# A streaming encoder step on one core: filling TensorE's opening and taking the first forget and query products feature by feature

## The reference

```python
x = layer_norm(x, ln_in_g, ln_in_b)
proj = einsum('btd,dn->btn', x, w_in)
q, f_pre, i_v, g_o, u_a, u_b, gate_a, gate_b = split(proj)
logf = log_sigmoid(f_pre) + log1p(lb * exp(-f_pre))   # 8 heads of 128 columns
...                                                   # gated recurrence over blocks of 64 frames
mix = (sigmoid(gate_a) * A + sigmoid(gate_b) * B) @ w_out
x = layer_norm(alpha * x + mix)
x = layer_norm(alpha * x + moe(x))                    # 16 experts, the best 2 of one group
```

## Time and profile before

| | us |
|---|---|
| median of 3 runs | 857.52 (857.51 to 860.41) |
| profiled execution | 857.89 |
| its span | 856.0 |
| TensorE busy | 812.6 (95%) |
| VectorE busy | 423.0 (49%) |
| ScalarE busy | 239.4 (28%) |
| GpSimd busy | 84.2 (10%) |

### The profile page before, as it was taken

One profiled execution on the slowest core, in us unless ns is written; L12 is line 12 of the kernel. 1 busy time (PEld: TensorE's weight loads), 2 busy tenths in 40 slices (PEclk: granted clock), 3 DMA queues, 4 the chain that ended last, 5 costly groups with the idle time before them and its releaser, 6 DMA issues.

```text
span 856.0 us, 12979 instructions
## 1 busy us (share of the span) xinstructions
PE 812.6 (95%) x5068; PEld 525.3 (61%) x5068; DVE 423.0 (49%) x706; ACT 239.4 (28%) x378; POOL 84.2 (10%) x146
## 2 busy tenths in 40 slices
PE   3999999999999999999999999999999999998892
PEld 2988888999999976577353443534435344352261
DVE  6788889988999984886010211202112021120137
ACT  5656666564454436111102010000100001000011
POOL 1354445530000100000000000000000000000000
PEclk8899999999999999999999999999999999999996
DMA  8422222334444844549999999999999999999991
GB/s 320 165 84 85 83 83 83 107 135 150 148 147 147 336 155 158 234 153 407 425 427 426 427 426 429 426 427 425 427 426 427 427 429 425 428 424 428 429 382 66
DMA packets 33883, 251.16 MB, mean 293 GB/s; under 512 B 4974, under 2 KB 8430, under 8 KB 21674
## 3 DMA queue, kind: packets, MB, share of 16 engines
q1 hardware_dynamic: 31296, 249.18, 71.5%
q10 hardware_dynamic: 2538, 1.32, 0.5%
HBM read 247.99 MB, written 2.48 MB: 293 GB/s over the span
## 4 chain that ended last, share of the span: by engine, by line
PE 57%; DVE 20%; DMA 10%; ACT 9%; issue 2%; ACTq 1%; DVEq 0%; SPq 0%
PE ps L539 56%; DMA ring<-in_w_up_e 8%; DVE ar L1798 5%; DVE ring L1676 4%; DVE split_t L1805 3%; ACT ring L1211 2%; ACT ar L1221 1%; DVE ar L1712 1%; ACT split_w L1130 1%; DMA out_new_conv_sample<-ar 1%; DVE ar L1723 1%; PE ps L939 1%; DVE ar L1667 1%; DMA ar<-in_x_prompt 1%; ACTq L1260 1%
## 5 line engine op out<-in xcount | busy, mean ns | idle before, releaser
L539 PE MATMUL ps<-ring,ar 128*64 128x512 f32 (+1 forms) x976 | 202.0, 567 | 1.6 <-DMA ring<-in_w_up_e 1.4
L539 PE MATMUL ps<-ring,xT 128*64 128x512 f32 (+2 forms) x848 | 149.5, 451 | 5.4 <-DMA ring<-in_w_gate_e 3.8
L539 PEld LDWEIGHTS ps<-ring,ar 128*64 128x64 f32 x976 | 67.9, 137 | 121.1 <-issue 111.8
L539 PEld LDWEIGHTS ps<-ring,xT 128*64 128x64 f32 (+1 forms) x848 | 75.2, 153 | 72.5 <-issue 62.6
L539 PE MATMUL ps<-split_x,split_t 128*128 128x320 f32 x672 | 101.0, 310 | 0.4 <-DVE split_t L1805 0.4
L539 PEld LDWEIGHTS ps<-split_x,split_t 128*128 128x128 f32 x672 | 98.6, 188 | 2.4 <-issue 1.6
L2108 DVE TENSOR_TENSOR ar<-ar,ps 128x512 f32<-128x512 f32 (+1 forms) x42 | 28.7, 684 | 135.8 <-PE ps L539 134.0
L539 PE MATMUL ps<-split_x,split_w 128*128 128x320 f32 x480 | 80.1, 322 | 4.1 <-DVE split_w L1636 1.2
L539 PEld LDWEIGHTS ps<-split_x,split_w 128*128 128x128 f32 x480 | 73.4, 194 | 7.4 <-ACT split_x L1165 2.1
L1798 DVE SCALAR_TENSOR_TENSOR ar<-ar,params 128x350 f32<-128x350 f32 x116 | 68.7, 592 | 4.1
L539 PE MATMUL ps<-ar 128*64 128x512 f32 (+7 forms) x424 | 66.7, 342 | 2.8 <-DVE mid L1741 2.8
(11 more groups left out here) (233 smaller groups left out, 862.7 us busy)
## 6 DMA issues: line engine op xcount, KB each, us to landing
ring<-in_w_gate_e SPq DMA_DIRECT2D x29, 2048.0 KB, 22.6
ring<-in_w_up_e SPq DMA_DIRECT2D x29, 2048.0 KB, 18.6
ring<-in_w_down_e SPq DMA_DIRECT2D x22, 2048.0 KB, 18.9
ring<-in_w_in SPq DMA_DIRECT2D x56, 512.0 KB, 4.4
ar<-in_w_down_e SPq DMA_DIRECT2D x4, 1792.0 KB, 20.1
ring<-in_w_down_end SPq DMA_DIRECT2D x3, 2048.0 KB, 36.0
ar<-in_w_up_e SPq DMA_DIRECT2D x3, 1792.0 KB, 15.7
ring<-in_w_o_a SPq DMA_DIRECT2D x8, 512.0 KB, 5.5
```

The source lines that it names most:

```text
L539: return pe.matmul(out, lhsT, rhs, start=start, stop=stop)
```

## The change

Five edits, all in the opening:

- TensorE issues fill products (`ones` by `ones`, 128x128, float32, into unused columns of bank 7): 40 before anything else, 10 after the first tile's transposes, 1 after the second's, 20 before the last transpose of the last tile, and 16 between the first head's value projection and the second head's forget products.
- `first_f` becomes `first_fq`: for each feature block the three forget products and two of the three query products, then what is left of the query.
- `X_COPIES` gives VectorE five T blocks (1, 2, 5, 6, 7) where it had three (1, 3, 6).
- GpSimd's subtraction waits for the last tile's norm too (`x0_ready` at 2).
- The two small steps on `lb` and `olb` stand further back on VectorE, ahead of L4.

```diff
-X_COPIES = ("T1", "T3", "L0", "L1", "T6", "L2", "L3", "L4", "L5", "L6", "L7")
+X_COPIES = ("T1", "T2", "T5", "L0", "L1", "L2", "L3", "T6", "T7", "L4", "L5", "L6", "L7")
+WARM = 40
...
+            pe.wait_ge(setup_done, 1)
+            for _ in range(WARM):
+                mm(ps[:, KT - 1, T:T + P], ones, ones, True, True)
             pe.wait_ge(ident_in, 16)
             for t, (ready, value) in enumerate(((x0_mid, 2), (x0_ready, 1), (x0_ready, 2))):
                 t0, n = TILES[t]
                 pe.wait_ge(ready, value)
                 for k in range(KT):
+                    if t == 2 and k == KT - 1:
+                        for _ in range(20):
+                            mm(ps[:, k, T:T + P], ones, ones, True, True)
                     last = pe.transpose(ps[:, k, t0:t0 + n], x0[0:n, t, k * P:(k + 1) * P], ident[0:n, 0:n])
                     if t == 2:
                         last.then_inc(x0T_done, 1)
+                for _ in range((10, 1, 0)[t]):
+                    mm(ps[:, KT - 1, T:T + P], ones, ones, True, True)
...
-            def first_f():
-                for k in range(KT):
-                    pe.wait_ge(xh_ready, XH[k])
-                    if k == 0:
-                        pe.wait_ge(xh_ready, XT_A[0])
-                    mm(ps[:, 0, 0:T], wh[:, k * P:k * P + P], xhk[:, k, :], k == 0, False)
+            def first_fq():
+                pe.wait_ge(wlo_ready, 1)
                 for k in range(KT):
                     pe.wait_ge(xl_ready, XL[k])
+                    mm(ps[:, 0, 0:T], wh[:, k * P:k * P + P], xhk[:, k, :], k == 0, False)
                     mm(ps[:, 0, 0:T], wh[:, k * P:k * P + P], xlk[:, k, :], False, False)
-                pe.wait_ge(wlo_ready, 1)
+                    last = mm(ps[:, 0, 0:T], wl[:, k * P:k * P + P], xhk[:, k, :], False, k == KT - 1)
+                    if k < KT - 1:
+                        mm(ps[:, 1, 0:T], wh[:, D + k * P:D + k * P + P], xhk[:, k, :], k == 0, False)
+                        mm(ps[:, 1, 0:T], wh[:, D + k * P:D + k * P + P], xlk[:, k, :], False, False)
+                last.then_inc(h["f_done"], 1)
+                mm(ps[:, 1, 0:T], wh[:, 2 * D - P:2 * D], xhk[:, KT - 1, :], False, False)
+                mm(ps[:, 1, 0:T], wh[:, 2 * D - P:2 * D], xlk[:, KT - 1, :], False, False)
+                pe.wait_ge(wlo_ready, 2)
                 for k in range(KT):
-                    last = mm(ps[:, 0, 0:T], wl[:, k * P:k * P + P], xhk[:, k, :], False, k == KT - 1)
-                last.then_inc(h["f_done"], 1)
+                    last = mm(ps[:, 1, 0:T], wl[:, D + k * P:D + k * P + P], xhk[:, k, :], False, k == KT - 1)
+                last.then_inc(h["q_done"], 1)
...
                 cur_v(*cur, first, bool(pprev))
+                if first:
+                    for _ in range(16):
+                        mm(ps[:, KT - 1, T:T + P], ones, ones, True, True)
...
             pool.wait_ge(whi_ready, 1)
+            pool.wait_ge(x0_ready, 2)
...
-            step(dve.tensor_tensor(lb[:, :], hv[:, 0:8], hv[:, 0:8], ALU.subtract))
-            signal(dve, dve.tensor_scalar(olb[:, :], lb[:, :], -1.0, 1.0, ALU.mult, ALU.add), setup_done, 2)
```

More of the change, by code:

```diff
@@ L664, in head_turn @@
                 if first:
-                    first_f()
+                    first_fq()
                 else:
                     cur_f(*cur, first)
-                if first or first_prev:
+                if first_prev:
                     cur_q(*cur, first)
@@ L1620, in _ @@
             dve.wait_ge(params_in, 16)
-            step(dve.tensor_tensor(lb[:, :], hv[:, 0:8], hv[:, 0:8], ALU.subtract))
-            signal(dve, dve.tensor_scalar(olb[:, :], lb[:, :], -1.0, 1.0, ALU.mult, ALU.add), setup_done, 2)
             for j, c in enumerate(X_COPIES):
                 k = int(c[1])
+                if c == "L4":
+                    step(dve.tensor_tensor(lb[:, :], hv[:, 0:8], hv[:, 0:8], ALU.subtract))
+                    signal(dve, dve.tensor_scalar(olb[:, :], lb[:, :], -1.0, 1.0, ALU.mult, ALU.add), setup_done, 2)
                 if c[0] == "T":
```

## The result

| | before | after |
|---|---|---|
| median of 20 runs each | 857.92 (857.20 to 860.41) | 860.39 (859.26 to 861.97) |
| profiled execution | 857.89 | 859.26 |
| its span | 856.0 | 857.4 |

The ratio is 1.0027, 95% interval 1.0021 to 1.0033. The change costs 1.8 to 2.8 us: a loss that is small, but clear of the noise of 20 runs each. Forecast were 859.1 us and +1.55, with a range of 851.6 to 861.2, or 857.8 to 861.0 without the rivals.

The account below looks back on a forecast made before the run. The opening was taken as bound by a chain of waits through one engine at a time, up to the second head's products. +1.25 and +0.3 summed to +1.55 us on the median 857.52: 859.1 us, range 851.6 to 861.2.

Parts of the forecast that it names:

- Price of a fill, 0.228: TensorE's float32 fill product: two records of 0.114 us each, so 0.228 us at full clock and 0.43 at 1.2 GHz.
- First fills end at 12.7: Opening on TensorE: 40 fills from 1.65, 10 slow until the clock rises at 5.85, 30 at 0.228, ending at 12.7.
- Norm of the last tile 0.8 us, ready at about 12.0, nobody there to use it: VectorE with GpSimd waiting: tile ready at 12.0 to 12.2 instead of 14.0, worth nothing since TensorE comes at 17.0.
- First copy 17.4, last remainder 25.8: Feature copies on ScalarE and VectorE: first starts at 17.4, 2.9 us later than before; last remainder at about 25.8.
- Forget products from 22.1, forget step 27.95, +1.25: First head: the 38th product ends at 27.9, ScalarE's first step behind it at 27.95 instead of 26.70, +1.25 us.
- The rival in which the copies are late: Feature copies, not TensorE, hold the forget gate, which comes at 24.3, 2.4 us earlier: 855.1 us, chance 0.08.
- Second head's products 38.35, +1.55: Behind the value projection: 16 fills hold TensorE until 38.35 instead of 38.06, +0.3 us more, sum +1.55.
- The two small steps, nothing: The lb steps moved back on VectorE: 0.34 us, needed by ScalarE only after feature 7, so worth nothing.
- The shift reaches the end 1:1: From the opening to the kernel's end: a shift at the second head's products is carried in full to the end.
- The late-clock rival: Opening on TensorE: clock low through all 40 first fills, which end at 18.8, 6.1 later: 865.2 us, chance 0.07.
- The cheap-fill rival: A fill takes one record's 0.114 us, so ScalarE starts 5.2 to 5.6 earlier than 26.70: 851.9 us, chance 0.16.

Follow-up runs that it names:

- halved fills: The changed kernel with 20, 5, 0, 10 and 8 fills instead of 40, 10, 1, 20 and 16: 853.74 us, ratio 0.9952 against the kernel before.
- The run with 80 fills: The changed kernel with 80 fills ahead of everything instead of 40, the other fills kept: 869.56 us, ratio 1.0131 against the kernel before.
- with the small steps in front: The kernel with halved fills, its two small lb steps back in front of VectorE's feature copies: 855.18 us, ratio 0.9969 against the kernel before.
- the kernel with three T blocks: The kernel with halved fills, with three T blocks on VectorE (1, 3, 6) as before instead of five: 853.77 us, ratio 0.9951 against the kernel before.

## Why the prediction was right, and where its steps were off

1. *Price of a fill, 0.228.* Shown: 80 records for 40 fills, and 9.00 to 9.22 us for 40 more, 0.225 to 0.231.
2. *First fills end at 12.7.* 12.07; the clock rose before 5 us where I had taken 5.85. Each us there was priced at 0.47, so the 0.6 us puts the rise at about 4.5, as an estimate. My range for it began at 5.1 (1.65 + 3.4) and missed it.
3. *Norm of the last tile 0.8 us, ready at about 12.0, nobody there to use it.* 0.80, ready at 11.83, TensorE there at 16.37. In the changed kernel worth nothing; with halved fills 1.65 us.
4. *First copy 17.4, last remainder 25.8.* 16.76 and 25.11, so 8.35 apart where I had 8.4.
5. *Forget products from 22.1, forget step 27.95, +1.25.* 21.81, 27.74, +1.04. Here two errors partly cancel: the start was 0.6 us too late, and the way from the last tile's first transpose to the products took 5.44 us (16.37 to 21.81) where I had 5.1. The rival in which the copies are late needed fewer fills; the halved kernel comes near that case: its products wait 0.45 us for the fifth remainder, until 18.80, and then run through.
6. *Second head's products 38.35, +1.55.* 38.09, +1.28: 16 fills from 34.50 to 38.3, then the products without an idle gap. VectorE's low part of the weights ended at 37.78, 1.03 later than before (36.75), so the fills held TensorE by some 0.25 more, where I had 0.3.
7. *The two small steps, nothing.* Wrong as a price of the edit, right for the sum as far as the trace tells: GpSimd ends at 14.38, and the first copy comes only 2.4 us later, at 16.76. The changed kernel was not run without it. Undone beside halved fills it costs 1.4 us.
8. *The shift reaches the end 1:1.* The run with 80 fills shows it for the medians: 9.22 at the second head, 9.00 to 9.17 at the end. A single profiled execution can't show it to better than 1 or 2 us. In that of the changed kernel +1.28 was +0.51 at 709.67 (709.16 before) and +1.4 at the end; in halved fills without GpSimd's wait -2.40 at the second head was -0.64 at 708.52, and with 80 first fills +10.50 was +11.63 at 720.79. The expert load that follows, in the changed kernel:

```profile
709.67 11.53 PE ps L540 x60
721.21 33.99 DMA ring<-in_w_up_e
755.24 9.21 PE ps L540 x64
```

That load took 33.99 us where it took 33.09. It is the longest of all here: the eleven experiments had 32.26 to 33.84, in no order that follows their openings. So I take such swings to belong to the execution and not to the change, which isn't shown.

What came out too small is the sum itself, at the median: +2.47 where I had +1.55, while the two profiled executions differ by +1.37. So the mechanism is confirmed step by step in the profiles, and about 1 us of the median is not. I had also taken 4.3 us as the least that a measurement can tell from no change; the 20 runs tell 2.5. Of the 1.3 us between 859.1 and 860.39, 0.4 is the base, 857.52 from 3 runs and 857.92 from 20. For the rest there are candidates, and none is shown:

- The profiled execution of the changed kernel was the fastest of its 20, so it stands for them badly.
- In the profiled execution before, ScalarE's norm of tile 0 began at 7.85; in the twelve others it began at 7.39 to 7.70. An execution of the kernel before with an early input can gain by it, one of the changed kernel can't, since its fills hold TensorE until 12.07. That would be up to 0.4 us.
- A clock that rises later than before 5 us would make an execution slower, by 0.47 us for each us. No profile here caught such a one in the changed kernel.
- The swings of single executions on the way to the end, as in point 8.

The late-clock rival did not happen. The cheap-fill rival fell on the price, but its timeline was that of a kernel worth having: 87 fills would fit the gaps if one took 0.114 us, and half as many at 0.228 do fit.

## What to carry to other kernels

A fill that keeps TensorE's clock up is work in an ordered queue: count its passes from a row of the same type (a float32 product here is two records), and size it so that TensorE still waits a little for its data. In this kernel fills paid where they ended about when the data came: half of each group (43 fills instead of 87) turned +2.5 us into -4.3, and no fills at all gave only -1.3. When two engines hinder each other, moving one step only moves the stall to the next instruction that can be hindered, so look at what stands there.

## What the runs showed of the hardware

- TensorE's clock column reads 1.00 from the start of every profile here, while the first transposes of the kernel before, 0.215 us apart where the same form takes 0.11 later, ran at half pace, so at 1.2 GHz. Counts of records per us are the better clock there.
- After 3.28 us of idle TensorE the clock fell and 48 products took 1.54 us more (8.85); after 1.28 us, in the halved kernel, it did not (7.31). Behind gaps of 1.67 and 1.72 us, in the kernels without GpSimd's wait and with the small steps in front, it stood at 0.50 too.
- GpSimd's tensor_tensor held VectorE's SBUF-to-SBUF tensor_scalar until its end: 2.60 us for 64x1024 (0.80 free) and 2.31 for 128x8 (0.17 free). Copies out of PSUM beside the same subtraction ran at their usual pace, three in 1.90 us, and a subtraction with two SBUF inputs that began beside it took 1.01 us instead of 0.49: in the kernel with three T blocks, the first of two such.

```profile
12.02 2.36 POOL L1514 TENSOR_TENSOR split_w<-ring,split_w 128x1024 fp32r<-128x1024 f32 x1 [11.57 <-ACT split_w L1146]
13.72 1.01 DVE L1649 TENSOR_TENSOR split_x<-xT,split_x 128x320 fp32r<-128x320 f32 x1
14.77 0.49 DVE L1649 TENSOR_TENSOR split_x<-xT,split_x 128x320 fp32r<-128x320 f32 x1
```

These are rows of that kernel's timeline: GpSimd works until 14.38. The GPSIMD Engine Reference in the Trainium skill (section 1, Specifications) names contention with VectorE instructions "in a 2-port perf mode or with two SBUF inputs". The trace agrees for the subtraction, which has two SBUF inputs. The `tensor_scalar` has one; whether it ran in such a mode, the profile doesn't say. What the rows add is that it lasts until the GpSimd instruction ends. Whether the subtraction is slowed or held for a part, one row doesn't tell.
